# Five plain gate and up pairs for six, and T sums formed in place with low parts made by adding transfers

## The reference

```python
h = rmsnorm(x, norm_mix_pre)
x = x + rmsnorm(hybrid_mixer(h, ...), norm_mix_post)     # attention heads and a gated recurrence
h = rmsnorm(x, norm_ffn_pre)
g = causal_dwconv(h @ w_gate, conv_ffn_w, conv_ffn_b)    # 2048 -> 6144, 3 taps
y = (gelu(g) * (h @ w_up)) @ w_down                      # 6144 -> 2048
x = x + rmsnorm(y, norm_ffn_post)
```

## Time and profile before

| | us |
|---|---|
| median of 3 runs | 2140.17 |
| lowest, highest | 2139.59, 2140.45 |
| the profiled execution, its own time | 2141.82 |
| its span | 2140.0 |
| TensorE busy | 2123.7 |
| VectorE busy | 1683.7 |
| ScalarE busy | 1020.9 |
| GpSimd busy | 342.4 |

### The profile page before, as it was taken

How to read it: one execution, slowest core, us unless ns; L and a number is a source line. 1 busy time by engine, 2 the same in 40 slices (tenths; PEclk the granted TensorE clock), 3 DMA queues, 4 the chain that set the end, 5 groups by cost and what they waited for, 6 DMA issues and landing times.

```text
span 2140.0 us, 44257 instructions
## 1 busy us (share of the span) xinstructions
PE 2123.7 (99%) x18238; PEld 2093.5 (98%) x18238; DVE 1683.7 (79%) x2297; ACT 1020.9 (48%) x1287; POOL 342.4 (16%) x428
## 2 busy tenths in 40 slices
PE   9999999999999999999999999999999999999998
PEld 8999999999999999999999999999999999999997
DVE  7777777778855887888888888888887867767876
ACT  6555554456422554444444444444453545445543
POOL 0222222222100001212112121111211001012002
PEclk9999999999999999999999999999999999999999
DMA  5788998879543446887888888788889648679645
GB/s 178 163 195 203 215 206 183 188 194 200 148 133 95 154 118 186 221 225 207 221 214 221 224 210 220 215 223 221 230 219 280 191 156 288 176 190 278 205 138 187
DMA packets 238754, 423.84 MB, mean 198 GB/s; under 512 B 17008, under 2 KB 151792, under 8 KB 237312
## 3 DMA queue, kind: packets, MB, share of 16 engines
q0 software_dynamic: 88224, 159.97, 36.2%
q1 hardware_dynamic: 147776, 256.84, 36.1%
q10 hardware_dynamic: 2592, 4.72, 0.6%
HBM read 382.64 MB, written 89.16 MB: 220 GB/s over the span
## 4 chain that ended last, share of the span: by engine, by line
PE 94%; DVE 2%; issue 1%; ACT 1%; POOL 1%; DMA 1%; POOLq 0%; DVEq 0%; ACTq 0%
PE bank L2087 30%; PE bank L2088 29%; PE bank L2089 29%; PE bank L2471 2%; PE bank L2166 1%; PE bank L2179 1%; DMA act_lo_f<-t_spill 1%; ACT w_all L775 0%; PE bank L2191 0%; PE bank L2190 0%; DVE w_all L1226 0%; ACT act_hi L1144 0%; PE bank L2251 0%; PE bank L2143 0%; POOL act_lo_f L766 0%
## 5 line engine op out<-in xcount | busy, mean ns | idle before, releaser
L2087 PE MATMUL bank<-act_hi,w_all 128*128 128x256 f32 x3272 | 909.4, 278 | 3.4 <-DVE up L1951 1.4
L2089 PE MATMUL bank<-act_hi,w_all 128*128 128x256 f32 x3272 | 903.8, 276 | 0.0
L2088 PE MATMUL bank<-act_lo,w_all 128*128 128x256 f32 x3272 | 903.7, 276 | 0.0
L2087 PEld LDWEIGHTS bank<-act_hi,w_all 128*128 128x128 f32 x3272 | 614.4, 188 | 8.7 <-issue 2.2
L2088 PEld LDWEIGHTS bank<-act_lo,w_all 128*128 128x128 f32 x3272 | 614.4, 188 | 0.7 <-issue 0.2
L2089 PEld LDWEIGHTS bank<-act_hi,w_all 128*128 128x128 f32 x3272 | 614.3, 188 | 0.0
L2087 PE MATMUL bank<-tsum,w_all 128*128 128x256 f32 x1280 | 353.5, 276 | 0.0
L2089 PE MATMUL bank<-tsum,w_all 128*128 128x256 f32 x1280 | 353.3, 276 | 0.0
L2088 PE MATMUL bank<-tsum,w_all 128*128 128x256 f32 x1280 | 353.3, 276 | 0.0
L1138 ACT ACTIVATE w_all<-raw_s 128x1024 fp32r<-128x1024 f32 x172 | 182.6, 1062 | 243.1 <-PE bank L2089 224.8
L1226 DVE TENSOR_TENSOR w_all<-raw,w_all 128x1024 fp32r<-128x1024 f32 x134 | 164.1, 1225 | 138.2 <-ACT w_all L775 136.6
(11 more groups left out here) (403 smaller groups left out, 3522.8 us busy)
## 6 DMA issues: line engine op xcount, KB each, us to landing
raw<-weights SPq DMA_DIRECT2D x262, 512.0 KB, 4.3
w_sums<-weights POOLq DMA_DIRECT2D x96, 512.0 KB, 6.9
raw_s<-weights SPq DMA_DIRECT2D x84, 512.0 KB, 5.7
raw_s<-weights POOLq DMA_DIRECT2D x84, 512.0 KB, 5.8
raw_a<-weights SPq DMA_DIRECT2D x66, 512.0 KB, 5.6
raw_s<-w_sums SPq DMA_DIRECT2D x48, 512.0 KB, 5.2
t_spill<-h_out POOLq DMA_DIRECT2D x48, 256.0 KB, 3.6
act_lo_f<-t_spill POOLq DMA_DIRECT2D x11, 1024.0 KB, 9.9
```

What stands on the lines that cost most here:

```text
L2087: pe.matmul(dst, ah, bh, start=start, stop=False, skip_group_check=goes_on)
L2088: pe.matmul(dst, ah, bl, start=False, stop=False, skip_group_check=goes_on)
L2089: return pe.matmul(dst, al, bh, start=False, stop=stop, skip_group_check=goes_on)
```

## The change

PLAIN goes from 6 to 5, so one plain pair becomes a fast one. T sums are formed in place over x1's quadrants, in the order of tiles 0, 1, 4, 5, 6, 7, 2, 3. ScalarE writes the high part and the negative of it (as the low part's first content), and two transfers on POOL's queue, 256 KB each, add x1 onto it, from SBUF to SBUF. Landing is counted in three parts: sums 0 and 1, sums 2 to 5, sums 6 and 7. The first fast pair's loads, its first high half, S2 and product (0, 1) wait for these. The square of the root moves from VectorE to ScalarE, T0 changes its place in tsum, some semaphores are merged, and the last bank choice follows the number of the last pair.

```diff
-PLAIN = 6
+PLAIN = 5
+T_ORDER = (0, 1, 4, 5, 6, 7, 2, 3)
+T_PART = (0, 0, 1, 1, 1, 1, 2, 2)
...
+        def t_lows(eng, part):
+            eng.wait_ge(lows_added[part], 32 * T_PART.count(part))
-        T0, T1, T2, T3 = [t_slot(t) for t in range(4)]
+        T1, T2, T3, T0 = [t_slot(t) for t in range(4)]
-        ADD_BANKS = (banks[2], banks[3], banks[4], banks[5], banks[7], banks[6])
+        ADD_BANKS = (banks[5], banks[6], banks[7], banks[2], banks[4], banks[3])
... SP: S1 loads of fast pairs 0 and 1, S3, A22
-                    sp.wait_ge(t_formed, 2 + 2 * i)
+                    t_lows(sp, 2 * i)
-                    sp.wait_ge(t_formed, 2)
+                    t_lows(sp, 0)
-                    sp.wait_ge(t_formed, 6)
+                    t_lows(sp, 1)
... POOL
-            for j in range(PLAIN - 2):
-                store_after(j)
+            def add_t(i):
+                k = T_ORDER[i]
+                pool.wait_ge(t_neg_done, i + 1)
+                for r in range(2):
+                    pool.dma_start(tsum[:, 2 * r:2 * r + 2, 1, k], in_two(x1[:, k + UK * r]).bitcast(F32R),
+                                   accum_op=ALU.add).then_inc(lows_added[T_PART[i]], 16)
+            for i in range(3):
+                add_t(i)
+            store_after(0)
+            store_after(1)
+            add_t(3)
+            add_t(4)
+            store_after(2)
+            add_t(5)
+            store_after(3)
             add_to_s1(0)
             add_to_s3(0)
-            store_after(PLAIN - 2)
+            add_t(6)
+            add_t(7)
             add_to_s1(1)
... ScalarE
-                act.activation(tsum[:, :, 0, k], sq[:].rearrange("p a (b n) -> p (a b) n", n=HS), ACT.Copy).then_inc(
-                    t_hi_done, 1)
+                act.activation(hi, formed, ACT.Copy)
+                act.activation(lo, formed, ACT.Copy, scale=-1.0).then_inc(t_neg_done, 1)
...
+            act.activation(acc[:], acc[:], ACT.Square, scale=(EPS * D / P) ** 0.5)
... first high half
-                    act.wait_ge(t_formed, 8)
+                    t_lows(act, 1)
... VectorE
-                at_least(dve, t_split, k)
-                chain(dve.tensor_tensor(t_f32[:, 1], b11, b12, ALU.subtract))
-                dve.tensor_tensor(t_f32[:, 2], b22, b12, ALU.subtract)
+                chain(dve.tensor_tensor(b11, b11, b12, ALU.subtract))
+                chain(dve.tensor_tensor(b12, b22, b12, ALU.subtract))
...
-            def t_lo(k):
-                dve.wait_ge(t_hi_done, k + 1)
-                dve.tensor_tensor(tsum[:, :, 1, k], t_f32, word(tsum[:, :, 0, k]), ALU.subtract).then_inc(t_split, 1)
...
+                if i == 0:
+                    t_lows(dve, 2)
                 wait_s1(dve, i)
... TensorE, fast pair 0
-                    pe.wait_ge(t_split, UK)
+                    for part in range(3):
+                        t_lows(pe, part)
```

More of the change, by code:

```diff
@@ L310, in block_kernel @@
             res_landed og_scaled x1_done x1_stored x1sq_done x1sum_ready
-            gate_taken tap_done conv_done gelu_done h_done x1_gained t_formed t_hi_done t_split
+            gate_taken tap_done conv_done gelu_done h_done x1_gained t_formed t_neg_done
             a11_landed a12_landed a22_landed s3_half s3_landed s2_done s4_done
@@ L347, in block_kernel @@
         t_landed = [sem(f"t_landed{n}") for n in range(7)]
+        lows_added = [sem(f"lows_added{n}") for n in range(3)]
         y_stored = [sem(f"y_stored{n}") for n in range(2)]
@@ L963, in _ @@
             split(10, 0, MORE_MIX)
[L964 removed]
+            act.wait_ge(lam_steps, 2)
             act.wait_ge(negc_stored, 16)
@@ L1053, in _, with gain_x1 @@
                 split(N_FF + 1 + m, (1 + m) % 2)
-            def gain_x1(k):
+            def gain_x1(i):
+                k = T_ORDER[i]
                 act.wait_ge(act_split, AFTER_Y + k + KT // 2 + 1)
@@ L1059, in gain_x1, with t_hi @@
                 ins.then_inc(x1_gained, 1)
-            def t_hi(k):
-                act.wait_ge(t_formed, k + 1)
-                act.activation(tsum[:, :, 0, k], sq[:].rearrange("p a (b n) -> p (a b) n", n=HS), ACT.Copy).then_inc(
-                    t_hi_done, 1)
+            def t_hi(i):
+                k = T_ORDER[i]
+                act.wait_ge(t_formed, i + 1)
+                formed = x1[:, k::UK].rearrange("p a (b n) -> p a b n", n=HS)
+                hi, lo = [tsum[:, :, part, k].rearrange("p (a b) n -> p a b n", b=2) for part in range(2)]
+                act.activation(hi, formed, ACT.Copy)
+                act.activation(lo, formed, ACT.Copy, scale=-1.0).then_inc(t_neg_done, 1)
             def last_tap(j):
@@ L1212, in _ @@
             act.wait_ge(sum_done, 6)
-            act.activation(cols[:, 0], banks[0][:, 0:QT], ACT.Sqrt, scale=1.0 / D).then_inc(root_done, 1)
+            act.activation(cols[:, 0], banks[0][:, 0:QT], ACT.Sqrt, scale=1.0 / D).then_inc(std_done, 1)
             for n, t in enumerate(ADD_BY_PE):
@@ L1825, in _ @@
             t_after(0)
-            t_lo(2)
+            t_form(3)
             taps(1)
@@ L1836, in _ @@
             t_after(2)
-            t_form(3)
+            t_form(4)
             taps(3)
             split(N_FF + 17, 1)
-            t_lo(3)
+            t_form(5)
             up_tile(3, SB[2], open_used(3, 1))
             t_after(3)
-            t_form(4)
             split(N_FF + 18, 0)
-            t_lo(4)
-            t_form(5)
+            t_form(6)
             split(N_FF + 19, 1)
-            t_lo(5)
-            gate_in(4, PJ[0], open_used(4, 0))
-            t_form(6)
-            taps(4)
-            split(N_FF + 20, 0)
-            t_lo(6)
-            t_form(7)
-            up_tile(4, PJ[1], open_used(4, 1))
-            t_after(4)
-            split(N_FF + 21, 1)
-            t_lo(7)
-            dve.scalar_tensor_tensor(out=acc[:], in0=acc[:], scalar=EPS * D / P, in1=acc[:], op0=ALU.mult, op1=ALU.mult)
-            split(N_FF + 22, 0)
-            split(N_FF + 23, 1)
+            t_form(7)
+            t3_of_pair(1)
             def product_lo(i, n):
@@ L2013, in add_y_square @@
                 dve.tensor_tensor(acc[:], acc[:], sq[:, 1], ALU.add).then_inc(yacc_added, 1)
-            gate_in(PLAIN - 1, PT[0], N_FAST - 2)
+            gate_in(PLAIN - 1, PJ[0], N_FAST - 2)
+            lo(0, 0)
             form_s2(0)
-            lo(0, 0)
             taps(PLAIN - 1)
@@ L2036, in _ @@
                 if i == 0:
-                    up_tile(PLAIN - 1, PT[1], N_FAST)
+                    up_tile(PLAIN - 1, PJ[1], N_FAST)
                 elif i <= NS:
                     fast_h(j - 1, i - 1)
-                if i <= NS:
+                if 0 < i <= NS:
                     t_after(j - 1)
@@ L2441, in _ @@
             tile(N_FF + 18, PJ[1])
-            pe.wait_ge(gate_taken, 2)
-            tile(N_FF + 20, PT[0])
-            pe.wait_ge(h_done, 2)
-            tile(N_FF + 22, PT[1])
             def fast_product(i, n, region, start):
@@ L2485, in _ @@
                 else:
-                    pe.wait_ge(gate_taken, (1, PLAIN)[i])
+                    pe.wait_ge(gate_taken, (1, 2)[i])
                 one_product(i, 0, a, True)
@@ L2490, in _ @@
                 else:
-                    pe.wait_ge(h_done, (1, PLAIN)[i])
+                    pe.wait_ge(h_done, (1, 2)[i])
                 if i == 0:
-                    pe.wait_ge(t_split, UK)
+                    for part in range(3):
+                        t_lows(pe, part)
                 one_product(i, 1, b, True)
```

48 lines of the change are left out of this document (20 added, 28 removed).

## The result

The changed kernel takes **2156.88 us** (median of 4 runs, 2155.95 to 2157.38), the kernel before 2140.31 on the same chip (2139.59 to 2140.45). The ratio is 1.0078, with an interval of 1.0066 to 1.0090: slower by 16.6 us, where 14.8 was forecast. The profiled execution has a span of 2154.2 us and is the fastest of its runs (2155.95); before, the span was 2140.0. Its trace is ahead of the one of before by about 1.0 us at 707 us already, and by 1.6 us when unit 17 ends (818.75 - 5.41 = 813.34 for 814.98), so times of the two are compared with this lead in mind.

What follows compares the result with a forecast made beforehand. TensorE's list of matmuls was taken to bound the kernel. Saving, two waits and clock gave 2140.17 - 2.72 + 4.1 + 11.6 + 1.7 = 2154.9, given as 2155 us, range 2146 to 2162.

Steps and rivals of the forecast that it cites:

- The price of an add: On POOL's queue, the two adding transfers of one T sum together hold all 16 DMA engines for 3.2 us.
- The rival with the plain rate: T adds move at the plain transfer rate, with waits of 2.4 and 8.4 us: 2148 to 2150 us, chance 0.20.
- Stall one: TensorE waits 4.1 us before plain unit 18, as the t3 store stands behind T adds on POOL's queue.
- Stall two: TensorE waits 11.6 us before product (0,1), as the last T low parts land late, at 840.5.
- The clock: After the 11.6 us gap on TensorE the granted clock drops, costing 1.7 us once; nothing for the 4 us gap.
- The saving of 2.7 us: On TensorE, turning plain pair 5 into a fast one, 21.76 to 19.04 us, gives 2.72 us back.
- No third stall: After product (0,1) the loads have run ahead, so TensorE meets no further new wait.
- The sum: Whole kernel: 2140.17 - 2.72 + 4.1 + 11.6 + 1.7 = 2154.9, given as 2155 us (+0.7%).

Runs made afterwards that it cites:

- e1_t3_first: Changed kernel with the t3 store moved ahead of the adds of T sum 4 on POOL; 2153.71 us, +13.7 against the kernel before.
- e2_adds_first: Changed kernel with the adds of T sums 6 and 7 moved ahead of the add to S3 on POOL; 2153.80 us, +13.7 against the kernel before.
- e12_both: Changed kernel with the t3 store ahead of T sum 4's adds, and T sums 6 and 7's adds ahead of the wait for S3; 2152.55 us.
- e6_kept_busy: Changed kernel with useless matmuls on TensorE, 24 before unit 18 and 88 before product (0,1); 2154.59 us, +14.4 against the kernel before.
- e10_four_adds: Changed kernel with T sums 0 to 3 by adding transfers, the other four low parts by VectorE, its list reordered; 2138.36 us, ratio 0.9991.
- e8_six_adds_ahead: Changed kernel, six plain pairs, t3 store ahead of T sum 4's adds, T sums 6 and 7's adds ahead of the S1 and S3 waits; 2141.69 us.
- e4_six_plain: Changed kernel with six plain pairs instead of five, all else as changed; 2158.11 us, +18.1 against the kernel before.
- e7_six_plain_order: Changed kernel, six plain pairs, t3 store ahead of T sum 4's adds, T sums 6 and 7's adds ahead of the S3 wait; 2148.60 us.

## Why the prediction came out right

- **The place of both stalls: right, and so are the causes named, with unequal weight.** TensorE waits at unit 18 and at product (0,1) and nowhere else new. The t3 store behind the adds is the whole cause of the first: e1_t3_first took it away. The T adds behind S3's wait on POOL are a part of the second: e2_adds_first left 5.1 of 8.0 us. The other part is the adding queued ahead of the last T sum, which the forecast counted too (three times 3.2 us), and which e12_both leaves standing alone.
- **The price of an add, 3.2 us: right.** In the full stretch 829:839 of the changed kernel, q0 shows

```profile
q0 software_dynamic: 1232, 1.57, 93.1%
```

  for three times 0.52 MB (T sums 6 and 7 and the add to S3): 0.931 x 10 / 3 = 3.1 us. In 775:788, where loads took another 27%, it was 3.6. The rival with the plain rate falls with it: even plain copies cost 2.2, and with them the time is still +12.7.
- **Stall one: 4.1 forecast, 5.4 measured.** The lead taken off, unit 18 came 1.3 us later than reckoned. The store's 6.0 us in the queue are as reckoned (6.1), and so is POOL's time for the two adds ahead of it, 0.71 each for 0.74. What is late is the chain in front of them. The lead of 1.6 us is TensorE's alone; VectorE's taps of pair 3, from which the chain starts, were only 0.6 us ahead (ended at 805.07 for 805.64):

```profile
804.32 0.75 DVE L1755 SCALAR_TENSOR_TENSOR cv<-gb,par,cv 128x512 f32<-128x512 f32 x1
```

  So T sum 4's copies ended at 807.64, where 808.4 less the lead is 806.8. That is 0.8 of the 1.3 us; the rest are steps of 0.3 us before POOL's first add and behind the store's landing.
- **Stall two: 11.6 forecast, 8.0 measured.** The low half that ends it was there at 842.8 for 844.3, and the last T lows at 838.9 for 840.5: both right, the lead taken off, but by luck, since the parts of the second miss and cancel: the S3 load went out at 819.01, 1.1 us late with the lead taken off, but took 6.4 us for the 8.6 reckoned, and from its landing to the last T lows it took 13.5 us for 12.4. What is off is TensorE's arrival: 834.9 for 832.7, or 3.8 us later when the lead is counted. 1.3 of them are the longer stall one, 2.4 the low clock under units 18 and 19, which the forecast had left out.
- **The clock: 1.7 forecast, 4.7 in the rows.** This is the step that was too small. I took the loss from the earlier trace rows once, and nothing for the gap of 5 us; both gaps brought the clock down, for 2.4 and 2.3 us. The two errors lean on each other: the first 2.4 us came out of stall two, and e6_kept_busy, 2.3 us faster, fits the second 2.3 us alone being in the time.
- **The saving of 2.7 us: in keeping, not shown alone.** The runs with no wait left stand at -2.1 with five plain pairs (e10_four_adds) and at +0.8 with six and a wait of 1.6 (e8_six_adds_ahead); the difference of 2.9, less that wait, is 1.3, with intervals about 2 us wide on either side.
- **No third stall: right.** From product (0,1) on no wait in the list is new.
- **The sum.** 2155 for 2156.88: stalls and clock were forecast as 17.4 and are 18.1 in the rows. That they come so near owes something to luck too: stall one was 1.3 us too small, the clock 3.0 too small and stall two 3.6 too large.

What the forecast did not see is that neither mending alone would do. The two reorderings alone leave +12.3; giving time alone leaves +18.1 (e4_six_plain); both together leave +8.4 (e7_six_plain_order), and with the adds ahead of S1's wait as well, +0.8. Open is how far the remaining wait of 10.2 us in e12_both is the rate of the adds and how far what the 16 engines move beside them: the landing of 13.9 us may hold both, and no run separates them.

## What to carry to other kernels

Work that is moved from a compute engine to transfers is paid on the 16 engines and in the issuing queue; look at both in the stretch where it lands, and ask of each instruction in that queue what it waits for, since everything behind it waits too (the T adds of e4_six_plain, ready at 825 us, went out at 848). If a full engine needs relief, move only as much as fills the idle time on the other side: against the kernel before, four of eight T sums by adds gave -2.1 us, none +0.8, eight +16.6 in the order of the changed kernel and +12.3 in that of e12_both. A gap on TensorE costs more than its length, as long as no later wait takes the slow stretch up.

## What the runs showed of the hardware

- The record of an adding transfer of 256 KB from SBUF to SBUF in pieces of 1 KB lasts 1.2 to 3.1 us on POOL, that of a plain copy of the same shape 0.7 to 1.1, that of a load with add of 512 KB 0.8 to 0.9. But behind an add as behind a copy, the next instruction starts after 0.7 us: read the starts, not the length.
- Two such transfers (512 KB) take 3.1 to 3.6 us of all 16 engines, as copies 2.2. The add from SBUF to SBUF is about as dear as the one that reads DRAM (3.4 by the earlier trace rows) or writes it (3.0 by the earlier trace rows).
- The last T add, behind a full queue, landed after 10.3 to 14.9 us with five plain pairs (10.5 in the changed kernel), where the median of its adds is 5.6 and the least 3.8.
- The granted clock fell to 1.2 GHz behind a gap of 5.4 us and behind one of 8.0, and the matmuls stayed 0.21 us apart for 4.8 and 4.6 us; with matmuls of no use in the gaps it did not fall.
